# Sample attention of a decoder step: weights, weighted sum and merge products in another order on TensorE

## What is computed

```python
# fox_sample, per sequence b: 2048 cached tokens in 16 pages, 8 new ones, 8 heads of 64
s_past = einsum('bqhd,bkhd->bhqk', q, kp) * scale + suffix + cn
s_new  = einsum('bqhd,bkhd->bhqk', q, k)  * scale + cn - cn
p = softmax(concatenate([s_past, causal(s_new)]))
o = einsum('bhqk,bkhd->bqhd', p[..., :past], vp) + einsum('bhqk,bkhd->bqhd', p[..., past:], v)
# merge_branches, here for the prompt's tokens
m = sigmoid(ga) * (a_out @ w_up_a) + sigmoid(gb) * (b_out @ w_up_b)
```

## Time and profile before

| | |
|---|---|
| runs, us | 1942.95, 1944.81, 1945.47 (median 1944.81) |
| the profiled execution | 1937.64 us, its span 1936.0 us |
| TensorE / VectorE / ScalarE / GpSimd busy | 93% / 31% / 15% / 10% |
| mean granted clock of TensorE | 0.966 |
| the sample stage | from 729.07 us (first load of biases) to 973.37 us (last instruction of VectorE) |
| its scores start, sequence 0 to 7 | 762.1, 777.9, 798.4, 820.4, 858.7, 880.1, 905.0, 925.5 |

### The profile page before, as it was taken

One profiled execution on the slowest core, in us unless ns is written; L12 is line 12 of the kernel. 1 busy time (PEld: TensorE's weight loads), 2 busy tenths in 40 slices (PEclk: granted clock), 3 DMA queues, 4 the chain that ended last, 5 costly groups with the idle time before them and its releaser, 6 DMA issues. The chain is left out here.

```text
span 1936.0 us, 22976 instructions
## 1 busy us (share of the span) xinstructions
PE 1794.6 (93%) x8703; PEld 909.1 (47%) x8703; DVE 605.0 (31%) x1216; ACT 284.2 (15%) x506; POOL 196.3 (10%) x286
## 2 busy tenths in 40 slices
PE   7999999899999993869899998999999999996996
PEld 4454454456566661434455444544444444442442
DVE  4201124343434334646321225211111111110677
ACT  2000001132222223213210113200000000000000
POOL 2000004200000002313300000100000000000331
PEclk9999999899999997879999998999999999998998
DMA  7102110532121218999741144799999999996242
GB/s 277 16 20 71 47 49 1 200 142 71 46 71 46 71 63 285 313 330 371 298 163 55 65 179 191 277 376 417 428 417 421 428 414 418 421 426 266 87 134 94
DMA packets 118817, 409.68 MB, mean 212 GB/s; under 512 B 23001, under 2 KB 46106, under 8 KB 106418
## 3 DMA queue, kind: packets, MB, share of 16 engines
q1 hardware_dynamic: 93906, 330.21, 44.5%
q0 software_dynamic: 16496, 56.15, 7.9%
q10 hardware_dynamic: 8304, 21.84, 2.8%
HBM read 357.36 MB, written 50.79 MB: 211 GB/s over the span
## 5 line engine op out<-in xcount | busy, mean ns | idle before, releaser
L2155 PE MATMUL psum<-arena 128*64 128x512 f32 (+1 forms) x1024 | 341.1, 595 | 1.4 <-DVE arena L2249 1.4
L853 PE MATMUL psum<-arena 128*128 128x363 f32 (+1 forms) x768 | 255.5, 478 | 4.3 <-ACT arena L884 4.2
L2155 PEld LDWEIGHTS psum<-arena 128*64 128x64 f32 (+1 forms) x1024 | 129.0, 163 | 179.1 <-issue 177.3
L853 PEld LDWEIGHTS psum<-arena 128*128 128x128 f32 x768 | 140.5, 192 | 78.6 <-ACT arena L884 6.7
L2194 PE MATMUL psum<-arena 128*64 128x512 f32 (+1 forms) x512 | 170.0, 595 | 1.0 <-DVE arena L2263 1.0
L1614 PE MATMUL psum<-arena 128*128 128x512 f32 x256 | 116.0, 609 | 1.9 <-PEq L1435 1.9
L2501 PE MATMUL psum<-arena 128*128 128x512 f32 x256 | 114.0, 603 | 1.4 <-DVE arena L2538 1.4
L2194 PEld LDWEIGHTS psum<-arena 128*64 128x64 f32 (+1 forms) x512 | 66.1, 163 | 101.9 <-issue 101.9
L305 PE MATMUL psum<-arena 128*128 128x512 f32 x256 | 111.9, 594 | 0.0
L2249 DVE TENSOR_TENSOR arena<-psum,g_moe_rows 128x1024 f32<-128x1024 f32 x24 | 29.4, 1225 | 250.4 <-PE psum L2149 250.4
L1160 PE MATMUL psum<-arena 128*128 128x512 f32 x160 | 76.4, 622 | 18.4 <-DVE arena L1326 16.3
(11 more groups left out here) (295 smaller groups left out, 1810.8 us busy)
## 6 DMA issues: line engine op xcount, KB each, us to landing
arena<-in_w_exp_gate SPq DMA_DIRECT2D x32, 2048.0 KB, 13.6
arena<-in_w_exp_up SPq DMA_DIRECT2D x32, 2048.0 KB, 14.7
arena<-in_w_exp_down SPq DMA_DIRECT2D x32, 2048.0 KB, 10.7
arena<-in_cache_k SPq DMA_DIRECT2D x128, 256.0 KB, 6.1
arena<-in_cache_v POOLq DMA_DIRECT2D x128, 256.0 KB, 7.6
moe_out<-arena ACTq DMA_DIRECT2D x24, 512.0 KB, 11.8
arena<-in_w_in SPq DMA_DIRECT2D x5, 2048.0 KB, 20.0
moe_out<-arena SPq DMA_DIRECT2D x1, 10240.0 KB, 34.8
```

The costliest lines, as they stand in the source:

```text
L853: done = mm(c.bank[7][:, 0:b - a], WG[blk % 2][:, k, q * P:(q + 1) * P], HT[:, k, a:b], start=(k == 0), stop=(k == KD - 1))
L2155: last = mm(out[rows_, :], XT[:, u % 2, k, rows_], c.ring_tile(LOAD[kind, u, r])[:, k, :], start=(k == 0), stop=(k == KD - 1))
```

## The change

In `values_between` TensorE now transposes all four chunks of weights, then the own ones, then takes the whole weighted sum, and only then the products A and B, one right after the other. VectorE's list is fitted to it: three chunks of keys instead of one are turned ahead of `merge_a`, and one instead of three ahead of `merge_b`. Nothing is added or removed, no semaphore count changes.

```diff
             def values_between(b, p):
 
-                turn_weights(b, 0)
-                turn_weights(b, 1)
+                for q in range(NCH):
+                    turn_weights(b, q)
+                turn_own(b)
+                weigh(b, range(NCH))
+                weigh_own(b)
                 up_piece(p, 0)
-                turn_weights(b, 2)
-                turn_weights(b, 3)
-                turn_own(b)
-                weigh(b, (0, 1))
                 up_piece(p, 1)
-                weigh(b, (2, 3))
-                weigh_own(b)
...
                 lowest(b)
                 if b + 1 < DB:
-                    turn_keys(b + 1, 0)
+                    for ch in range(NCH - 1):
+                        turn_keys(b + 1, ch)
                 if b >= 1:
                     merge_a(b)
                 if b + 1 < DB:
-                    for ch in range(1, NCH):
-                        turn_keys(b + 1, ch)
+                    turn_keys(b + 1, NCH - 1)
                 if b >= 1:
                     merge_b(b)
```

## The result

| | before | changed |
|---|---|---|
| median of 20 runs, us | 1940.77 (1932.0 to 1947.41) | 1952.76 (1947.88 to 1959.93) |
| ratio | | 1.0075, 95% interval 1.0062 to 1.0089 |
| profiled execution, span | 1937.64, 1936.0 | 1951.79, 1950.2 |
| sample stage: scores 1 to scores 7 | 147.6 | 151.8 |
| scores 7 to the first matmul of the next stage | 50.4 | 56.3 |

A forecast was written before the change was run, and what follows sets the result against it. Key loads were taken to pace the middle, TensorE's own list dense steps and the tail. Terms 5.9 - 5.5 + 2.7 + 1.8 + 0.3 = +5.2 us on the median 1944.81 gave 1950.0; range 1941.8 to 1956.

The forecast's parts named there:

- (a): Tail: second product waits for VectorE to multiply the first out of the shared bank, three times 0.85, +2.55 us.
- (b): Tail: the third turn of weights waits for its bank until ScalarE has copied, 2 x 0.2, +0.4 us.
- (d): Stage's end: VectorE's merge operations after the last product are no longer hidden behind the weighted sum, +1.7 us.
- (e): Tail: the 3.69 us wait for step 6's values and the slow product after it go away, -5.5 us.
- (c, f): Tail: TensorE waits at the turns for copies behind the gate's sigmoids, +1.25, plus one late transfer, +2.7 us.
- (g): Tail: TensorE standing still at the turns likely brings one spell at the low clock, +1.8 us.
- part 3: Middle of the sample stage, to the last scores: step growth mostly hidden by key waits, net about +0.3 us.
- the credit of 3.4 us for the filled holes: Middle: values' loads starting some 4 us earlier at 787 and 867 fill idle DMA time, 3.4 us of transfer early.
- Part 1: Paired products: the second waits 0.85 us each step; where keys are late it runs beside the fourth chunk's wait.
- rival 3: Keys and values both later: middle +3.75, last values at 943; +11 us, 1955.8; chance 0.14.
- Rival 1: Absorbed: step 6's values and gate column land in time, clock stays up; +0.7 us, 1945.5; chance 0.26.
- rival 2: Not slower: filled holes at 787 and 867 start the last scores earlier; -3.2 us, 1941.6; chance 0.10.

The follow-up runs named there:

- run 1: Changed kernel with ScalarE's two sigmoids of a gate column moved behind the next sequence's exponentials; 1953.85 us, ratio 1.0078 to the kernel before.
- run 12: VectorE's new order throughout, TensorE's new order in the last two values' steps alone; 1946.99 us, ratio 1.0034 to the kernel before.
- run 7: Changed kernel with VectorE's old order (one key chunk ahead of the multiplication, three behind); 1947.13 us, ratio 1.0053 to the kernel before.
- run 3: Changed kernel with the old order in the last two values' steps only; 1939.79 us, ratio 1.0006 to the kernel before.
- run 4: Changed kernel with the next values' first two chunks issued only after product A, the last two after product B; 1959.77 us, ratio 1.0115 to the kernel before.
- run 5: Changed kernel with VectorE turning two key chunks ahead of product A's multiplication and two behind; 1953.2 us, ratio 1.0082 to the kernel before.
- run 6: Kernel before with VectorE's new order alone, TensorE's order unchanged; 1933.48 us, ratio 0.998 to the kernel before.
- run 8: Kernel before with the weighted sum in one piece and product B behind it, product A still between the turns; 1948.58 us, ratio 1.0068.
- run 9: Kernel before with product B behind the whole sum, and the next values' second half issued only after product B; 1944.78 us, ratio 1.0032.
- run 10: Changed kernel with the second half of the next values issued only after product A; 1949.08 us, ratio 1.0059 to the kernel before.
- run 11: Kernel before with VectorE's new order throughout and TensorE's new order in the first step alone; 1933.63 us, ratio 0.9975 to the kernel before.

## Why the prediction was right in kind and short in size

**Pair waits (a).** Right. Forecast 3 x 0.85, measured 0.85, 0.88 and 0.85 us.

**Turns (b).** Right within a tenth or two. Sixteen transposes in one piece took 2.45 us in a dense step, where the two pieces of eight took 1.32 and 1.04 before: +0.1 for +0.2.

**The end (d).** Right. Forecast +1.7; the last transposed result waited 2.23 us, and 0.53 in the timeline of before.

**The old wait goes away (e).** Right for the profile of the changed kernel, where the tail has no wait for values; runs 1 and 12 show that it only gives way to the gate wait and comes back when that is gone.

**The gate and the late transfer (c, f).** Right in kind, and in that the two overlap; the size was off. 1.25 + 2.7 = 3.95 us was forecast, 6.11 measured. The column landed 8 us later, not 2.7. SyncE issued its gate loads only 1.3 us later than before (918.6 and 919.9 for 917.3 and 918.6), but all sixteen value loads now go out beside them (from 916.50 in one row; before, eight from 918.50 and eight from 923.99). That these are what delayed the column was not tested by itself.

**The clock (g).** Right: 0.9 us at the turns and 0.9 at the sum, 1.9 for 1.8.

So the tail was forecast at +4.9 and came out at +5.9 in the profiles (56.3 for 50.4).

**The middle (part 3).** This is the step that failed: +0.3 forecast, +4.2 measured in the profiles (151.8 for 147.6), a little beyond its own upper end of 3.75. The other profiles with TensorE's new order in the middle have +0.5 (run 7) to +7.5 (run 3), leaving out run 4, which held the values back. The term that was wrong is the credit of 3.4 us for the filled holes. Scores 6 started 2.8 us later than before (907.75 for 904.97), and the last key chunk of that step was there 2.8 us later: the 2.7 us that I charged for values ahead of keys, and nothing to set against them. The dense step behind it grew by 1.3 us where 1.05 were forecast. The values did gain from their earlier release, the keys did not. From scores 1 to scores 7 the queue of the values moved 23.6 MB for 21.6 before, the queue of keys, columns and weights 27.9 for 28.5. Here the rule of the Trainium skill (DMA: Bandwidth & Descriptors, Queues, rings and completion order) that each DMA engine takes packets in turn from the queues with work fits better than my credit; no run isolates it. Without that credit the middle would have been +3.75, close to the 4.2 measured.

Part 1 was right about late keys: the second product ran beside the wait for the fourth chunk, and the scores still waited 0.73 us for it. Run 5 confirms that nothing is gained when B waits less. The sign that I named for rival 3, waits for keys at the scores that shrink by less than the steps grow, misled: they shrank by 17 us, since the same late keys now held up B and the late gate column the turns.

Early values alone do not make keys late. In run 7 the queue of the values moved as much (23.9 MB) and VectorE waited 4.1 us for keys; in run 6 it waited 4.5. What these two have in common are even steps (24 to 29 and 23 to 27 us) and DMA engines that are taken throughout the middle (353 and 359 GB/s for 341), with a middle of 148 us. I had taken the pace of the transfers as given; it depends on when the loads are released. Why even steps help was not taken apart further.

Two more signs of the prediction came out just beyond their ends: scores 7 started at 929.6 (922 to 929 was given), and the stage ended 10 us later (2 to 9).

**Outside the stage.** Nothing was forecast there, and the profiles differ by 4.2 us (964.3 for 960.1). The twelve other profiles have 959.1 to 964.6 us for the same code, with no relation to the edit, so I take this as scatter between executions. It leaves a gap: the stage grew by 10 us in the one pair of profiles, and the ratio gives 14.5. Whether the stage costs more in the other executions could not be seen, since each kernel has one profile.

**The rivals.** Rival 3 (keys and values both later) came nearest: +11, with the middle at its upper end and one transfer wait of 5. Rival 1 fell with the gate wait; rival 2 had the hole at 790 filled, but the last scores came at 929.6, not before 922. I gave rival 3 a chance of 0.14 on the ground that the total bytes are the same and start earlier; that is true, and beside the point, since it was the values that started earlier and the keys that were waited for.

**What stays open.** Why run 8, with the covers back, loses 13 us. Its middle is 153.9 us, and the early release in one row may be the cause, since run 9 gets about half back in the ratio; but its two lengths hold only 3.5 of the 13 us, and 9 and 10 did not restore the middle to 148, and a release in another pattern was not tried.

## What to carry to other kernels

Two pieces of work that share one buffer are cheap apart and dear together: between them stood the time that hid a hand-over of 0.85 us, a copy of 0.41 us and 3 us of a late transfer (TensorE's wait at the turns was 3.07 us in run 3 and 6.11 in the changed kernel). In a stage that transfers pace, ask of a reordering not only how much longer an engine's step gets but which load it releases earlier and which one that pushes back: here the values came free earlier and the keys were needed. And a longer list is paid in full where no wait for a load can hide it: the last steps of a loop deserve an order of their own (run 3, +1 us for +14.5).

## What the runs showed that I had not expected

- VectorE's half of the change alone makes the kernel faster, 0.998 (0.9966 to 0.9994), although TensorE waits 21.1 us in small pieces: the DMA engines move 359 GB/s over the middle instead of 341, and the tail has no wait for a transfer (44.3 us for 50.4). This version (run 6), with or without the first step of run 11 (0.9975, 0.9961 to 0.999), beats both kernels.
- TensorE can fall to the low level of its clock (1.2 GHz) after short pauses. In run 7 the scores followed five times on a wait of 1.83 us. Four times they took 5.84 to 6.01 us, at a mean granted clock of 0.71 to 0.73; at 874.74 they took 4.41, at 1.00. The same pause does or does not cost 1.5 us, and what decides it no run here shows.
